# Attention's heads laid in pairs over the 128 rows: scores by row halves, mixing by column halves, and the first scores and the samples' q moved

## The chip, the cores and the metric

The kernel runs on one core of a Trainium2 chip. The metric is the device time of one launch in microseconds (us), lower is better. The core has five engines with instruction queues of their own: TensorE (PE, its weight loads shown as PEld), VectorE (DVE), ScalarE (ACT), GpSimd (POOL) and the queue that issues most DMAs (SP). They work in parallel and hand over to each other by semaphores.

## What is computed

One inference step of a two-layer decoder for 512 prompt tokens and 8 samples of 8 new tokens (576 tokens, 1024 features). Layer 0 is a recurrent block, layer 1 is attention over a window of 128 tokens; each ends with a retrieval of experts that takes most of the time. The change touches the attention alone: 16 query heads of 64 features, 4 key/value heads (so four query heads share one), a rotary position code on q and k, and a learned sink per head.

```python
def swa_prompt(q, k, v, sinks):           # blocks of 128 tokens, keys of the block and of the one before
    ...
    s = jnp.einsum('bnqkgd,bnskd->bnkgqs', qb, kb).astype(jnp.float32) * scale
    p = sink_softmax(s, mask[None, :, None, None], sink)
    o = jnp.einsum('bnkgqs,bnskd->bnqkgd', p.astype(v.dtype), vb)
    return o.reshape(b, t, N_HEADS * HEAD_DIM)
```

`sink_softmax` takes the larger of the row's maximum and the sink, exponentiates, and divides by the sum with the sink's own term. The samples do the same against 128 cached keys and their own 8.

## The kernel before, in words

Every engine has its program written out by hand; what sets the order of the work is the order of the code of each engine, and the semaphores between them. There is no scheduler.

Attention comes in the middle of the launch. TensorE projects k (two tiles of 128 features, `D_K`), v, and then q (eight tiles, `D_Q`, L1632). As each tile of q comes out of PSUM, ScalarE makes a copy with the halves of each head exchanged (`rope_shift`, L894), and VectorE's `rope` (L1402) multiplies that copy by the sine (L1407), the tile by the cosine (L1408), and adds the two into `qR`: once for the even head in the tile's rows 0 to 63 (L1412) and once for the odd head in rows 64 to 127 (L1413). Both go to rows 0 to 63 of `qR`, which is 64 rows by 16 heads by 576 tokens. After the last tile VectorE copies the samples' part of `qR` to `qS` (L1429).

Then come 16 **units**, one for each of 4 blocks of 128 prompt tokens and 4 key/value heads, in a software pipeline. For unit u:

- TensorE `scores` (L1842): 4 matmuls of 64 rows by 128 columns of weights, one per head, over 256 keys (128 for the first four units), to two PSUM banks.
- VectorE `scale_max`: scales and masks the scores (L1443), takes the maximum (L1450), and three small steps. ScalarE takes the exponentials (L914). VectorE `normalise` (two small steps and L1467).
- TensorE `turn`: 8 transposes (L1882). ScalarE copies them to `prT` (L924).
- TensorE `mix` (L1886): one matmul of 64 columns of weights for each of two blocks of keys (one for the first four units), over 512 columns, that is, four heads of 128 queries (L1893). All four heads come out in rows 0 to 63 of PSUM.
- VectorE `keep` (L1470): two copies of 64 rows, the even heads to rows 0 to 63 of `xn`, the odd ones to rows 64 to 127 (L1474).

A turn of TensorE's loop holds the scores of unit u+2, the transposes of unit u, the mixing of unit u-1, and, from u = 8 on, the mixing of one sample (`sample_mix`, L1917 and L1919). A turn of VectorE's loop holds the normalising of u, the scaling of u+2, and the copy of u-1. Two further items, 4 and 5, carry the samples' scores through the same ring of score banks, and VectorE does the samples' maximum, normalising and copies at fixed units. After the last unit the output projection starts (L1632 again).

The matmuls on `qR`, `kR`, `prT` and `vtok` are in plain fp32; the profile shows each of them as two instructions (so the 4 matmuls of a unit's scores stand as x8).

Of the kernel before, what the change touches and what calls it, by code (L numbers as in the profile page):

```python
# [25 lines left out]
P = 128  # L26
# [220 lines left out]
def decoder(nc, xin, consts, params, wts, wv, stconv, kcT, kc, vc, uT, u, v,  # L247
            yT, convP, hOut, kNew, vNewP, vNewS, kKeep, vKeep, convS, gate_dram, s_dram):
    with ExitStack() as ctx:
# [65 lines left out]
        atc = st.take("atc", [P, C_N - C_COS])  # L315
        qR = st.take("qR", [HD, NH, T])
        kR = st.take("kR", [HD, NKV, T])
        qS = st.take("qS", [HD, NB, NH, TS])
# [110 lines left out]
        def _(spq):  # L429
# [94 lines left out]
            spq.wait_ge(sem("k_ready"), 2)  # L524
            spq.dma_start(kNew, kR[:, :, TP - WIN:T]).then_inc(sem("out_done"), 16)
            load_weights(W_Q + 2, W_O + 2)
# [430 lines left out]
        def _(dve):  # L957
# [443 lines left out]

            def rope(d0, n, dst):  # L1402
# [12 lines left out]

            def attention():
                dve.wait_ge(sem("atc_loaded"), 16)
                norm_stats(2)
                norm_apply(N_KV, X_KV)
                rope(D_K, 2, kR)  # L1420
                dve.wait_ge(sem("roped"), 2)
# [4 lines left out]
                norm_apply(N_AT, X_AT, inv=rinv[:, :])  # L1426
                rope(D_Q, NC, qR)
                dve.wait_ge(sem("roped"), 2 + NC)
                dve.tensor_copy(qS[:, :, :, :], qR[:, :, TP:T].rearrange("p h (b s) -> p b h s", b=NB)  # L1429
                                ).then_inc(sem("qS_ready"), 1)  # L1430
                ob = xn
                dve.wait_ge(sem("tile_done"), D_O)

                def scale_max(k, u):
# [12 lines left out]
                    if not n:  # L1447
# [3 lines left out]
                    chain.settle()  # L1451
                    sk = prm[:, P_SINK + kv * GRP:P_SINK + (kv + 1) * GRP]
                    chain.did(dve.tensor_tensor(m[:, 0, 0:GRP], m[:, 0, 0:GRP], sk, ALU.max))
# [3 lines left out]
                    dve.tensor_tensor(m[:, 3, 0:GRP], sk, m[:, 0, 0:GRP], ALU.subtract  # L1457
                                      ).then_inc(sem("pmax"), 1)

# [10 lines left out]
                def keep(u):  # L1470
                    n, kv = divmod(u, NKV)
                    dve.wait_ge(sem("p_out"), u + 1)
                    for e in range(2):
                        ins = dve.tensor_copy(  # L1474
                            ob[e * HD:(e + 1) * HD, 2 * kv:2 * kv + 2, n * WIN:(n + 1) * WIN],
                            ps[0:HD, OUT, :].rearrange("p (g e q) -> p g e q", g=2, e=2)[:, :, e])
                        if e == 0:
                            chain.did(ins)
                    ins.then_inc(sem("o_copied"), 1)

# [52 lines left out]
                for k in items_due(-1):  # L1533
                    item(k)
                for u in range(UNITS):
                    normalise(u)
# [34 lines left out]
        def _(pe):  # L1571
# [255 lines left out]
            def attention():  # L1827
# [10 lines left out]
                project(W_Q, D_Q, NC, X_AT)  # L1838
                pe.wait_ge(sem("roped"), 2 + NC)
                pe.wait_ge(sem("v_ready"), 1)  # L1840

                def scores(k, u):  # L1842
                    n, kv = divmod(u, NKV)
                    ks = max(0, n - 1) * WIN
                    lo = 0 if n else WIN
                    for g in range(GRP):
                        ins = pe.matmul(sbank(k)[:, g // 2, (g % 2) * 256 + lo:(g % 2 + 1) * 256],
                                        qR[:, kv * GRP + g, n * WIN:(n + 1) * WIN],
                                        kR[:, kv, ks:(n + 1) * WIN], start=True, stop=True)
                    return ins  # L1850

                def sample_scores(k, h):
# [3 lines left out]
                    for b in range(4 * h, 4 * h + 4):  # L1856
                        for kv in range(NKV):
                            o = sbank(k)[32 * kv:32 * kv + 32, b // 2 % 2, (b % 2) * 256:(b % 2) * 256 + WIN + TS]
                            q = qS[:, b, kv * GRP:(kv + 1) * GRP].rearrange("p g s -> p (g s)")
                            pe.matmul(o[:, 0:WIN], q, kc_sb[:, b, kv], start=True, stop=True)  # L1860
                            ins = pe.matmul(o[:, WIN:], q, kR[:, kv, TP + b * TS:TP + (b + 1) * TS],
                                            start=True, stop=True)
# [23 lines left out]
                def mix(u):  # L1886
# [154 lines left out]
```

## Time and profile before

| | us |
|---|---|
| median of 3 runs | 3170.84 |
| lowest and highest | 3169.39, 3171.84 |
| the profiled execution, its own time | 3175.33 |
| its span | 3173.5 |
| from the last matmul of q's projection to the first of the output projection | 1642.1 to 1787.6 |
| granted TensorE clock over the span | 0.979 of full speed |

Durations below are of the profiled execution. Positions are us from the start of its span. PE's busy time of the whole span is 3063.0 us (97%) and DVE's 2544.1 us (80%); only a small window of the span belongs to the change.

### The profile page before, as it was taken

Reading aid. Unit: us, or ns where it says so; the run is one execution under the profiler, and the core shown is the slowest. Engines: PE = TensorE matmul, PEld = TensorE weight load, DVE = VectorE, ACT = ScalarE, POOL = GpSimd, SP = SyncE. Lnnn points to the kernel's source line nnn. Section 1 sums busy time; section 2 is a strip of 40 time slices with the busy share of each in tenths; the row PEclk is TensorE's granted clock in tenths of the full one; section 3 lists DMA queues with packets and bytes.
Section 4 is the critical chain, followed back from the end, with each engine's and each line's share of the span. In section 5 each row is a group of like instructions: output and inputs, shape, how many; then the busy total and the mean of one; then the engine's idle time right before and its main releaser. Section 6 shows DMA issues by size and latency. Waiting matters only on the chain.

```text
span 3173.5 us, 50434 instructions
## 1 busy us (share of the span) xinstructions
PE 3063.0 (97%) x19070; PEld 2973.1 (94%) x19070; DVE 2544.1 (80%) x4947; ACT 1379.8 (43%) x2558; POOL 1882.1 (59%) x1165
## 2 busy tenths in 40 slices
PE   8889999999999999999988899999999999999998
PEld 7779999999999999999875789999999999999998
DVE  7755999977776899989567448999877759998997
ACT  2522344477774333333344233343677753333333
POOL 4543488887776665664130233788877766565651
PEclk9999999999999999999987899999999999999999
DMA  3212499999999999999130022899999999999994
GB/s 111 73 54 92 139 335 347 325 403 393 394 386 367 401 401 398 400 395 398 58 99 1 27 67 85 283 348 347 355 400 394 387 360 398 401 398 400 400 397 191
DMA packets 286337, 920.89 MB, mean 290 GB/s; under 512 B 27344, under 2 KB 77136, under 8 KB 282432
## 3 DMA queue, kind: packets, MB, share of 16 engines
q1 hardware_dynamic: 154080, 415.37, 35.9%
q0 software_dynamic: 111280, 404.77, 33.3%
q10 hardware_dynamic: 20736, 97.53, 7.6%
q8 instruction: 152, 2.49, 0.3%
q14 instruction: 89, 0.73, 0.1%
HBM read 817.07 MB, written 102.38 MB: 290 GB/s over the span
## 4 chain that ended last, share of the span: by engine, by line
PE 67%; DVE 21%; DMA 8%; issue 2%; POOL 1%; ACT 1%; SPq 1%; DVEq 0%; ACTq 0%
PE ps L1767 24%; PE ps L1709 15%; PE ps L1632 10%; PE ps L1712 7%; DMA sring<-s_dram 6%; PE ps L1743 5%; DVE xrest L1168 2%; DVE xl L975 1%; DVE xn L982 1%; DMA gt<-gate_dram 1%; DVE low L1336 1%; DVE cand L1251 1%; DVE cand L1258 1%; DVE rowsB L1161 1%; PE ps L1893 1%
## 5 line engine op out<-in xcount | busy, mean ns | idle before, releaser
L787 ACT ACTIVATE high<-raw 128x1024 fp32r<-128x1024 f32 x512 | 542.8, 1060 | 937.2 <-PE ps L1767 640.2
L629 POOL TENSOR_TENSOR low<-raw,high 128x1024 fp32r<-128x1024 f32 x256 | 614.8, 2402 | 157.6 <-ACT high L787 154.2
L1709 PE MATMUL ps<-xh,high 128*128 128x384 f32 x2048 | 701.4, 342 | 6.3 <-ACT sring L840 6.3
L1767 PE MATMUL ps<-hh,high 128*128 128x384 f32 (+1 forms) x2048 | 691.4, 338 | 7.6 <-DVE low L1336 7.4
L1767 PE MATMUL ps<-hl,high 128*128 128x384 f32 x2048 | 691.7, 338 | 0.0
L1767 PE MATMUL ps<-hh,low 128*128 128x384 f32 x2048 | 690.7, 337 | 0.0
L1709 PE MATMUL ps<-xl,high 128*128 128x384 f32 x2048 | 688.6, 336 | 0.0
L620 POOL DMA_INDIRECT rowsB<-v,pick x192 | 330.0, 1719 | 207.1 <-DVE xrest L1168 192.3
L620 POOL DMA_INDIRECT rowsA<-v,pick x192 | 315.1, 1641 | 213.8 <-DVE xrest L1168 206.5
L1712 PE MATMUL ps<-xh,low 128*128 128x384 f32 x2048 | 399.5, 336 | 7.2 <-POOL low L629 7.2
L1767 PEld LDWEIGHTS ps<-hh,high 128*128 128x128 f32 x2048 | 385.2, 188 | 11.6 <-DVE low L1336 11.4
L1709 PEld LDWEIGHTS ps<-xh,high 128*128 128x128 f32 x2048 | 388.2, 190 | 7.2 <-ACT high L787 6.9
L1709 PEld LDWEIGHTS ps<-xl,high 128*128 128x128 f32 x2048 | 388.3, 190 | 0.0
L1767 PEld LDWEIGHTS ps<-hh,low 128*128 128x128 f32 x2048 | 385.4, 188 | 0.7
L1767 PEld LDWEIGHTS ps<-hl,high 128*128 128x128 f32 x2048 | 385.6, 188 | 0.0
L1712 PEld LDWEIGHTS ps<-xh,low 128*128 128x128 f32 x2048 | 360.8, 189 | 8.3 <-POOL low L629 8.2
L1336 DVE TENSOR_TENSOR low<-raw,high 128x1024 fp32r<-128x1024 f32 x256 | 311.2, 1216 | 0.0
L1632 PE MATMUL ps<-xh,high 128*128 128x288 f32 x1152 | 254.5, 303 | 26.8 <-DVE xl L975 18.4
L1161 DVE SCALAR_TENSOR_TENSOR rowsB<-rowsB,ps 128x1024 f32<-128x1024 f32 x192 | 230.6, 1212 | 34.5 <-DMA rowsB<-u,pick 34.2
L840 ACT ACTIVATE sring<-ps 128x384 f32<-128x384 f32 x256 | 125.1, 488 | 297.4 <-PE ps L1712 296.9
L1168 DVE SCALAR_TENSOR_TENSOR xrest<-rowsA,phid,xrest 128x1024 f32<-128x1024 f32 x192 | 249.0, 1297 | 0.6
L1323 DVE TENSOR_TENSOR sring<-sring,gt 128x384 f32<-128x384 f32 x256 | 140.4, 550 | 135.7 <-DMA sring<-s_dram 82.7
(282 smaller groups left out, 5205.3 us busy)
## 6 DMA issues: line engine op xcount, KB each, us to landing
raw<-uT SPq DMA_DIRECT2D x256, 512.0 KB, 6.8
raw<-v SPq DMA_DIRECT2D x256, 512.0 KB, 14.0
gate_dram<-gblk ACTq DMA_DIRECT2D x24, 2048.0 KB, 11.6
s_dram<-sring ACTq DMA_DIRECT2D x120, 384.0 KB, 6.8
gt<-gate_dram SPq DMA_DIRECT2D x30, 1536.0 KB, 20.9
sring<-s_dram SPq DMA_DIRECT2D x120, 384.0 KB, 14.7
raw<-wts SPq DMA_DIRECT2D x74, 512.0 KB, 3.3
rowsB<-u,pick POOLq DMA_INDIRECT x192, 8.0
```

Of the source, the lines that this page charges most:

```text
L620: pool.indirect_dma_start(out=row_slot(k), out_offset=None, in_=u if k < S0 + S1 else v, in_offset=bass.IndirectOffsetOnAxis(ap=pick[:, c: ...
L629: pool.tensor_tensor(low[:, m % 4], raw[:, m % 4], high[:, (m + 2) % 3].bitcast(F32), ALU.subtract).then_inc(sem("lo_ready"), 1)
L787: act.activation(high[:, (m + 2) % 3], tile_raw(m), ACT.Copy).then_inc(sem("hi_ready"), 1)
L1161: dve.scalar_tensor_tensor(row, row, 1.0, wide(XS0 if k < S0 else XS1), ALU.mult, ALU.mult, accum_out=phid[:, c:c + 1]).then_inc(sem("row_ ...
L1168: dve.scalar_tensor_tensor(acc[c >= S0], row.rearrange("p (c d) -> p c d", d=P), phid[:, c:c + 1], acc[c >= S0], ALU.mult, ALU.add).then_i ...
L1323: dve.tensor_tensor(hb, hb, gt[:, n // GE % 2, :, n % GE * GB:(n % GE + 1) * GB], ALU.mult).then_inc(sem("h_mul"), 1)
L1336: dve.tensor_tensor(tile_low(m), tile_raw(m), high[:, (m + 2) % 3].bitcast(F32), ALU.subtract).then_inc(sem("vlo_ready"), 1)
L1632: ins = pe.matmul(ps[:, dbank(d) + h, 0:H2], m[:, c], x[:, c, h * H2:(h + 1) * H2], start=(c == 0 and j == 0), stop=(c == NC - 1 and j == 2))
L1709: pe.matmul(ps[:, m % 2, 0:DN], a[:, c], x[:, c, 0:DN], start=(c == 0 and k == 0), stop=False)
L1712: ins = pe.matmul(ps[:, m % 2, 0:DN], b[:, c], xh[:, c, 0:DN], start=False, stop=(c == NC - 1))
L1743: ins = pe.matmul(ps[:, 2 + g % 2, i * P:(i + 1) * P], hotB[:, k], hotA[:, k], start=True, stop=True)
L1767: ins = pe.matmul(ps[:, c, 0:cols], w[:, c], h[:, n % 3, 0:cols], start=opens, stop=(n == KEYS - 1 and j == 2))
```

## The change

`qR` and `kR` now fill all 128 rows. `qR` holds a pair of heads per tile as the projection leaves it: the even head in rows 0 to 63, the odd one in rows 64 to 127. So `rope` makes one addition of 128 rows per tile of q where there were two of 64. `kR` holds each key head twice, once in either half of the rows, which takes four additions per tile of k where there were two.

`scores` takes the even head of a pair from rows 0 to 63 and the odd one from rows 64 to 127, in turn, into two different PSUM banks. A unit's slots are thereby ordered even heads first, and the sinks are read in that order. `mix` makes two matmuls over 256 columns where there was one over 512: the even heads' output goes to rows 0 to 63 of PSUM, the odd heads' to rows 64 to 127. `keep` is then a single copy of 128 rows.

The wait of TensorE for the tiles of q, which was for all eight ahead of the first scores, is now for seven ahead of the scores of units 0 to 2 and for all eight ahead of those of unit 3. The samples' copy to `qS`, now two copies, stands on VectorE behind the scaling of units 0 and 1.

```diff
-        qR = st.take("qR", [HD, NH, T])
-        kR = st.take("kR", [HD, NKV, T])
+        qR = st.take("qR", [P, NC, T])
+        kR = st.take("kR", [P, NKV, T])
...
-                    chain.did(dve.tensor_tensor(dst[:, 2 * f], rc[0:HD, r], rot[0:HD, r], ALU.add))
-                    ins = dve.tensor_tensor(dst[:, 2 * f + 1], rc[HD:P, r], rot[HD:P, r], ALU.add)
+                    if d0 == D_K:
+                        for e in range(2):
+                            rows = slice(e * HD, (e + 1) * HD)
+                            for at in range(2):
+                                ins = dve.tensor_tensor(kR[at * HD:(at + 1) * HD, 2 * f + e], rc[rows, r], rot[rows, r],
+                                                        ALU.add)
...
+                    else:
+                        ins = dve.tensor_tensor(qR[:, f], rc[:, r], rot[:, r], ALU.add)
                     ins.then_inc(sem("roped"), 1)
...
-                dve.wait_ge(sem("roped"), 2 + NC)
-                dve.tensor_copy(qS[:, :, :, :], qR[:, :, TP:T].rearrange("p h (b s) -> p b h s", b=NB)
-                                ).then_inc(sem("qS_ready"), 1)
...
-                    for e in range(2):
-                        ins = dve.tensor_copy(
-                            ob[e * HD:(e + 1) * HD, 2 * kv:2 * kv + 2, n * WIN:(n + 1) * WIN],
-                            ps[0:HD, OUT, :].rearrange("p (g e q) -> p g e q", g=2, e=2)[:, :, e])
...
+                    dve.tensor_copy(ob[:, 2 * kv:2 * kv + 2, n * WIN:(n + 1) * WIN],
+                                    ps[:, OUT, 0:2 * WIN].rearrange("p (g q) -> p g q", g=2)
+                                    ).then_inc(sem("o_copied"), 1)
...
                 for k in items_due(-1):
                     item(k)
+                dve.wait_ge(sem("roped"), 2 + NC)
+                by_half = qS[:, :, :, :].rearrange("p b (f e) s -> p b f e s", e=2)
+                for e in range(2):
+                    ins = dve.tensor_copy(by_half[:, :, :, e], qR[e * HD:(e + 1) * HD, :, TP:T]
+                                          .rearrange("p f (b s) -> p b f s", b=NB))
...
-                pe.wait_ge(sem("roped"), 2 + NC)
                 pe.wait_ge(sem("v_ready"), 1)
...
-                    for g in range(GRP):
-                        ins = pe.matmul(sbank(k)[:, g // 2, (g % 2) * 256 + lo:(g % 2 + 1) * 256],
-                                        qR[:, kv * GRP + g, n * WIN:(n + 1) * WIN],
-                                        kR[:, kv, ks:(n + 1) * WIN], start=True, stop=True)
+                    if u < NKV:
+                        pe.wait_ge(sem("roped"), 2 + (NC - 1 if u < NKV - 1 else NC))
+                    for g in range(2):
+                        for e in range(2):
+                            ins = pe.matmul(sbank(k)[:, e, g * 256 + lo:(g + 1) * 256],
+                                            qR[e * HD:(e + 1) * HD, 2 * kv + g, n * WIN:(n + 1) * WIN],
+                                            kR[e * HD:(e + 1) * HD, kv, ks:(n + 1) * WIN], start=True, stop=True)
...
-                        ins = pe.matmul(ps[0:HD, OUT, :], vtok[:, n - 1 + kb, kv * HD:(kv + 1) * HD],
-                                        prT[:, u % 2, 4 * kb:4 * kb + 4].rearrange("p g q -> p (g q)"),
-                                        start=(kb == kbs[0]), stop=(kb == 1))
+                        for e in range(2):
+                            j = 4 * kb + 2 * e
+                            ins = pe.matmul(ps[e * HD:(e + 1) * HD, OUT, 0:2 * WIN],
+                                            vtok[:, n - 1 + kb, kv * HD:(kv + 1) * HD],
+                                            prT[:, u % 2, j:j + 2].rearrange("p g q -> p (g q)"),
+                                            start=(kb == kbs[0]), stop=(kb == 1))
```

Two places of the engines' own order show what stands in a row before and now. The first is VectorE at the end of q's rope: `rc` and `rot` are the two products, `pr` the scores of a unit, `sm` its small sums. Before:

```order
L1407 TENSOR_TENSOR rot<-rot,atc 128x576 [waits rot_ready]
L1408 TENSOR_TENSOR rc<-ps,atc 128x576
L1412 TENSOR_TENSOR qR<-rc,rot 64x576 [waits d_free,dve_chain]
L1413 TENSOR_TENSOR qR<-rc,rot 64x576
L1429 COPY qS<-qR 64x1024 [waits roped]
L1443 SCALAR_TENSOR_TENSOR pr<-ps,atc 128x4x128 [waits p_scores,tile_done]
L1448 MEMSET pr 128x4x128
L1450 TENSOR_REDUCE sm<-pr 128x4 [waits dve_chain]
```

And now, up to the normalising of unit 0:

```order
L1421 TENSOR_TENSOR qR<-rc,rot 128x576 [waits d_free,dve_chain]
L1448 SCALAR_TENSOR_TENSOR pr<-ps,atc 128x4x128 [waits p_scores,tile_done]
...
L1464 TENSOR_TENSOR sm<-prm,sm 128x4 [waits dve_chain]
L1540 COPY qS<-qR 64x64x8 [waits roped]
L1540 COPY qS<-qR 64x64x8
L1469 TENSOR_TENSOR sm<-sm 128x4 [waits pexp]
L1471 RECIPROCAL sm<-sm 128x4 [waits dve_chain]
L1473 TENSOR_TENSOR pr<-pr,sm 128x1024 [waits dve_chain]
```

One addition is gone from each tile of q, and the copy to `qS` has moved behind the scaling of two units.

The second is TensorE in a turn of the loop that holds a sample too (scores, transposes, mixing, then the sample's mixing). Before:

```order
L1847 MATMUL ps<-kR,qR 128x256 [waits pmax]
L1847 MATMUL ps<-kR,qR 128x256 x3
L1882 MATMUL ps<-cst,pr 128x128 [waits prT_ready,p_ready]
L1882 MATMUL ps<-cst,pr 128x128 x7
L1893 MATMUL ps<-prT,vtok 64x512 [waits o_copied,prT_ready]
L1893 MATMUL ps<-prT,vtok 64x512
L1917 MATMUL ps<-pssT,vc_sb 64x32
L1919 MATMUL ps<-pssN,vnew 64x32
```

And now:

```order
L1907 MATMUL ps<-prT,vtok 64x256 [waits o_copied,prT_ready]
L1907 MATMUL ps<-prT,vtok 64x256 x3
L1932 MATMUL ps<-pssT,vc_sb 64x32
L1934 MATMUL ps<-pssN,vnew 64x32
```

The scores and transposes stand as before (L1859 and L1894 now), and the two matmuls over 512 columns have become four over 256; no semaphore has moved in the loop.

## Rows read from the trace of the kernel before

**Rows 1.** The page's chain that ended last, shares of the span by engine.
```profile
PE 67%; DVE 21%; DMA 8%; issue 2%; POOL 1%; ACT 1%; SPq 1%; DVEq 0%; ACTq 0%
```

**Rows 2.** Stretches: length, busy PE, PEld, DVE, ACT, POOL, granted clock, DMA share, GB/s.
```profile
1642.10:1656.80 14.70, 5.85 (x24) 5.26 (x24) 10.11 (x19) 6.01 (x14) 3.38 (x2) 0.62 0.56 142
...
1656.80:1786.20 129.40, 111.50 (x560) 68.55 (x560) 88.09 (x174) 51.95 (x156) 0.00 (x0) 0.76 0.02 9
```

**Rows 3.** VectorE's waits in 1656.8 to 1786.2: total us, times, longest.
```profile
DVE xn L1474 <- PE ps L1893: 23.2, 11, 4.7
DVE pr L1443 <- PE ps L1847: 13.0, 9, 4.7
```

**Rows 4.** The chain at the start of the stage: start, us, what.
```profile
1644.72 1.54 DVE rot L1407
...
1647.81 0.77 DVE qR L1413
1648.62 2.09 PE ps L1847 x8
1650.81 0.69 DVE pr L1443
```

**Rows 5.** Timeline of VectorE: start, us, line, tiles, shape, [idle before, releaser].
```profile
1584.52 0.06 DVE L1424 MEMSET mark<- 128x1 f32 x1 [11.05 <-PE ps L1834]
...
1648.60 0.69 DVE L1429 COPY qS<-qR 64x1024 f32<-64x1024 f32 x1
```

**Rows 6.** VectorE's copies by line and shape: count, busy us, mean ns, idle before.
```profile
L1474 DVE COPY xn<-ps 64x256 f32<-64x256 f32 x32 | 13.3, 417 | 23.8 <-PE ps L1893 23.2
```

**Rows 7.** The chain in the units, at full and at half clock.
```profile
1740.73 1.92 PE ps L1847 x8
1742.65 1.02 PE ps L1882 x8
1743.68 1.86 PE ps L1893 x4
...
1755.88 0.35 PE ps L1919 x2
...
1756.93 3.71 PE ps L1847 x8
1760.64 1.90 PE ps L1882 x8
```

**Rows 8.** Another stretch of the chain: mixing at half clock.
```profile
1727.29 3.60 PE ps L1893 x4
```

**Rows 9.** Timeline of VectorE in the units: the long waits and one short.
```profile
1684.52 0.86 DVE L1474 COPY xn<-ps 64x256 f32<-64x256 f32 x2 [0.97 <-PE ps L1893]
...
1703.18 0.86 DVE L1474 COPY xn<-ps 64x256 f32<-64x256 f32 x2 [2.68 <-PE ps L1893]
...
1730.93 0.87 DVE L1474 COPY xn<-ps 64x256 f32<-64x256 f32 x2 [2.42 <-PE ps L1893]
...
1760.68 1.23 DVE L1443 SCALAR_TENSOR_TENSOR pr<-ps,atc 128x1024 f32<-128x1024 f32 x1 [4.71 <-PE ps L1847]
1765.74 0.86 DVE L1474 COPY xn<-ps 64x256 f32<-64x256 f32 x2 [1.99 <-PE ps L1893]
1772.96 0.87 DVE L1474 COPY xn<-ps 64x256 f32<-64x256 f32 x2 [4.69 <-PE ps L1893]
1780.06 0.87 DVE L1474 COPY xn<-ps 64x256 f32<-64x256 f32 x2 [4.57 <-PE ps L1893]
1783.61 0.87 DVE L1474 COPY xn<-ps 64x256 f32<-64x256 f32 x2 [2.68 <-PE ps L1893]
```

**Rows 10.** TensorE by line and shape (rows*columns of weights, then moving): count, busy us.
```profile
L1719 PE MATMUL ps<-cst,xn 128*64 128x128 f32 x64 | 6.7, 276 | 0.0
...
L1798 PE MATMUL ps<-xn,ones 128*32 128x128 f32 x128 | 3.9, 273 | 0.0
```

**Rows 11.** Timeline of weight loads: the first load of a mixing behind transposes.
```profile
1727.22 0.29 PEld L1893 LDWEIGHTS ps<-prT,vtok 128*64 128x64 f32 x2 [0.33 <-issue]
```

More of the change, by code:

```diff
@@ L524, in _ @@
             spq.wait_ge(sem("k_ready"), 2)
-            spq.dma_start(kNew, kR[:, :, TP - WIN:T]).then_inc(sem("out_done"), 16)
+            spq.dma_start(kNew, kR[0:HD, :, TP - WIN:T]).then_inc(sem("out_done"), 16)
             load_weights(W_Q + 2, W_O + 2)
@@ L1400, in experts, with rope @@
                 dve.memset(mark[:, :], 0.0).then_inc(sem("x_ready"), 1)
-            def rope(d0, n, dst):
+            def rope(d0, n):
                 for f in range(n):
@@ L1411, in rope @@
                     dve.wait_ge(sem("d_free"), d + 1)
-                    chain.did(dve.tensor_tensor(dst[:, 2 * f], rc[0:HD, r], rot[0:HD, r], ALU.add))
-                    ins = dve.tensor_tensor(dst[:, 2 * f + 1], rc[HD:P, r], rot[HD:P, r], ALU.add)
+                    if d0 == D_K:
[4 more added lines that the diff above has]
+                                                        ALU.add)
+                                if (e, at) != (1, 1):
+                                    chain.did(ins)
+                    else:
+                        ins = dve.tensor_tensor(qR[:, f], rc[:, r], rot[:, r], ALU.add)
                     ins.then_inc(sem("roped"), 1)
@@ L1419, in attention @@
                 norm_apply(N_KV, X_KV)
-                rope(D_K, 2, kR)
+                rope(D_K, 2)
                 dve.wait_ge(sem("roped"), 2)
@@ L1426, in attention @@
                 norm_apply(N_AT, X_AT, inv=rinv[:, :])
-                rope(D_Q, NC, qR)
-                dve.wait_ge(sem("roped"), 2 + NC)
-                dve.tensor_copy(qS[:, :, :, :], qR[:, :, TP:T].rearrange("p h (b s) -> p b h s", b=NB)
-                                ).then_inc(sem("qS_ready"), 1)
+                rope(D_Q, NC)
                 ob = xn
@@ L1451, in scale_max, with pairs @@
                     chain.settle()
-                    sk = prm[:, P_SINK + kv * GRP:P_SINK + (kv + 1) * GRP]
-                    chain.did(dve.tensor_tensor(m[:, 0, 0:GRP], m[:, 0, 0:GRP], sk, ALU.max))
+                    sk = prm[:, P_SINK + kv * GRP:P_SINK + (kv + 1) * GRP].rearrange("p (g e) -> p e g", e=2)
+                    def pairs(i):
+                        return m[:, i, 0:GRP].rearrange("p (e g) -> p e g", e=2)
+                    chain.did(dve.tensor_tensor(pairs(0), pairs(0), sk, ALU.max))
                     chain.settle()
@@ L1456, in scale_max @@
                     chain.settle()
-                    dve.tensor_tensor(m[:, 3, 0:GRP], sk, m[:, 0, 0:GRP], ALU.subtract
-                                      ).then_inc(sem("pmax"), 1)
+                    dve.tensor_tensor(pairs(3), sk, pairs(0), ALU.subtract).then_inc(sem("pmax"), 1)
                 def normalise(u):
@@ L1472, in keep @@
                     dve.wait_ge(sem("p_out"), u + 1)
-                    for e in range(2):
-                        ins = dve.tensor_copy(
-                            ob[e * HD:(e + 1) * HD, 2 * kv:2 * kv + 2, n * WIN:(n + 1) * WIN],
-                            ps[0:HD, OUT, :].rearrange("p (g e q) -> p g e q", g=2, e=2)[:, :, e])
-                        if e == 0:
-                            chain.did(ins)
-                    ins.then_inc(sem("o_copied"), 1)
+                    dve.tensor_copy(ob[:, 2 * kv:2 * kv + 2, n * WIN:(n + 1) * WIN],
+                                    ps[:, OUT, 0:2 * WIN].rearrange("p (g q) -> p g q", g=2)
+                                    ).then_inc(sem("o_copied"), 1)
                 def sample_scale(k, h):
@@ L1534, in attention @@
                     item(k)
+                dve.wait_ge(sem("roped"), 2 + NC)
[3 more added lines that the diff above has]
+                                          .rearrange("p f (b s) -> p b f s", b=NB))
+                    if e == 0:
+                        chain.did(ins)
+                ins.then_inc(sem("qS_ready"), 1)
                 for u in range(UNITS):
@@ L1860, in sample_scores @@
                             pe.matmul(o[:, 0:WIN], q, kc_sb[:, b, kv], start=True, stop=True)
-                            ins = pe.matmul(o[:, WIN:], q, kR[:, kv, TP + b * TS:TP + (b + 1) * TS],
+                            ins = pe.matmul(o[:, WIN:], q, kR[0:HD, kv, TP + b * TS:TP + (b + 1) * TS],
                                             start=True, stop=True)
```

## The prediction

> **What bounds the kernel now.** The chain that ended last is TensorE work for two thirds of the span [rows 1], but nearly all of it is projections and experts, which the change leaves alone. So I read only the window of attention. The table of stretches cuts it in two: a start of 14.7 us in which TensorE is busy for 5.85, and the 129.4 us of the 16 units, with TensorE busy 111.5, VectorE 88.1, ScalarE 52.0 and a mean granted clock of 0.76 [rows 2]. The clock has two levels, 2.4 and 1.2 GHz, so about half of the units' time runs at the lower one. The reader should see there that two engines share the lead: VectorE works 88 us and TensorE makes it wait. The list of waits gives the amount: 23.2 us for the mixing and 13.0 us for scores, in 20 waits, 36.2 us in all [rows 3]. ScalarE is behind both. The end of the stage is the last copy of VectorE, so the stage lasts as long as VectorE's work, plus those 36.2 us, plus the start.
>
> The chain in the units gives one turn of the loop at either level of the clock [rows 7, 8]: scores 1.92 us at full speed and 3.71 at half, transposes 1.02 and 1.90, mixing 1.86 and 3.60. A pair of the samples' small matmuls is 0.35 us at half speed, and there are 8 pairs in a turn.
>
> **The start.** q's last tile leaves TensorE at 1642.1. VectorE multiplies from 1644.72 (that start is set by ScalarE's copies), adds, and ends at 1648.58; only then do the scores of unit 0 run, 2.09 us at half clock for two units' worth, and VectorE's first scaling begins at 1650.81 [rows 4]. Now the scores of units 0 and 1 need tile 6 only, which is roped before the projection ends, so they run at 1642.1 while VectorE still works on tile 7. One of the two last additions goes, and scaling starts at 1647.81: 3.0 us earlier. An addition over 128 rows might cost 1.54 us, as the multiplication L1407 over 128 rows does [rows 4], and not 0.77; then 0.8 of the 3.0 goes back. I take 0.77, since the elements per row are the same as in the additions of 64 rows. The copy to qS took 0.69 us under the first scores, where it cost nothing [rows 5]; two halves of it, 0.75 with the gap, now stand on VectorE with no cover, ahead of the first normalising. The start gains 3.0 - 0.75 = **2.3 us**.
>
> The two added additions per tile of k are 4 x 0.77 = 3.1 us on VectorE. They lie ahead of a wait of 11.05 us for v's projection [rows 5] and cost nothing; without that cover they would cost 3.1. The seven other additions saved in q lie under the projection and gain nothing.
>
> **VectorE's copies.** A unit's two copies take 0.87 us together, and each 0.42 for 256 elements a row [rows 6, 9]. One copy of 128 rows has the same 256 elements: 0.42. That is 0.45 x 16 = **7.2 us** of VectorE work.
>
> **TensorE's halves.** The scores are still 4 matmuls of the same length. The mixing is twice as many, half as long, so the same sum if nothing overlaps: for both the lower bound of the gain is nothing. What the trace shows of matmuls side by side: instructions that all write the same column half take 6.7 us for 64, or 105 ns each; of the same 128 columns moved, those that change quarter each time take 3.9 us for 128, or 30 ns each [rows 10]. That is 3.4 to 3.5 of a possible 4, and 3.8 without the tail of the two groups. So column halves in turn should come to some 0.53 of the time: mixing 0.98 us for 1.86, and 1.9 for 3.60. For row halves no row exists; the bounds are 1.92 (none) and 0.96 (all), and I take 1.02 for the nearest case, the columns, and 1.95 at half clock. A turn thus saves TensorE 1.8 us at full and 3.5 us at half clock.
>
> **What is left of VectorE's waits.** Thirteen of the 20 are of 1.62 us or less and sum to 36.2 - 23.7 = 12.5; the other seven (2.68, 2.42, 4.71, 1.99, 4.69, 4.57, 2.68) sum to 23.7 [rows 9]. I take the clock as it was at each. The small ones go, except that the first units mix one block only, and a wait like the 0.97 at 1684.5 keeps some: 1.1 us left in all. The long ones lose the half of the mixing or the scores just before them: 1.74, 1.74, 1.8, 1.5, 1.4, 1.3, 0.9, leaving 0.9, 0.7, 2.9, 0.5, 3.3, 3.3 and 1.8, or 13.4. The last three are a chain of normalise, transpose, mix, copy with no scaling left to fill it, so they stay at any clock. VectorE arrives 0.43 us earlier at each of the seven, which adds 3.0. Left: 1.1 + 13.4 + 3.0 = 17.5, so **18.7 us** of waits go.
>
> **The sum** is 2.3 + 7.2 + 18.7 = 28.2 us. The profiled execution took 3175.3, which becomes 3147.1; it lay 4.5 above the median of 3170.84, so for the median I say **3142.6 us**. After attention nothing is changed: the output projection starts at half clock now and will again. VectorE becomes the engine that bounds a turn: 1.6 (normalise) + 3.0 (scale) + 0.45 (copy) = 5.1 us of work against TensorE's 1.0 + 1.0 + 1.0 and 1.8 for a sample.
>
> **Rivals.**
>
> *Row halves do not overlap*, column halves do. For it: both halves write all 128 rows of PSUM, and no row of this trace has such a pair. Against it: they go to two banks. Then TensorE saves only 0.9 or 1.7 per turn, the waits for scores (13.0) stay as they are and those for the mixing lose about 10 while VectorE comes earlier: gain 2.3 + 7.2 + some 6 = 15.5, **3155 us**. If neither overlapped, VectorE's earlier arrival would be given back at the 20 waits, up to 20 x 0.45 = 9.0 of 9.5: gain 0.5 to 4.
>
> *The clock stays at half.* TensorE has less to do per turn; in the start, where it was busy 5.85 of 14.7 us, it had 0.62 [rows 2]. At half clock throughout, a turn with a sample is 1.95 + 1.9 + 1.9 + 8 x 0.35 = 8.6 us against VectorE's 5.1, so 3.5 of wait in each of six turns, some 13 in the last two turns and the end, and 1.2 in each of the first eight (1.6 + 1.9 + 1.9 + 0.45 and handovers make 6.3): 21 + 13 + 10 = 44 to 49 in place of 36.2. The gain is 9.5 - 8 to 9.5 - 13: +1.5 to -3.5, **about 3171 us**. Against it: at half clock TensorE would be all but fully busy, and out of just such a stretch it came back: mixing took 3.60 us at 1727.3 and 1.86 at 1743.7 [rows 7, 8]. At full clock throughout only the last three waits and 2 us more stay, 8.5 in all: gain 2.3 + 7.2 + 27.7 = 37, **3134 us**.
>
> *Slower: each change of half empties the array.* The first weight load of a mixing behind the transposes stood idle for 0.33 us at half clock [rows 11]; if alternating halves paid that for each change, nothing would overlap, and a unit has six changes, so 16 x 6 x 0.33 = 32 us at half clock, half that at full, some 24. Less the 0.5 to 4 that is left without overlap, and with a part under VectorE's work: slower by about 15, **3186 us**. It decides from a price of 4 / 96 = 0.04 us a change. Against it: the quarters of [rows 10] change at every matmul and run at 30 ns. The Trainium skill, "TensorEngine Tiling (Array Packing)", section "Key Properties", says that changing the tiling mode drains TensorE, but not changing the tile. By that rule the change adds no drain between halves; the trace's 30 ns agree.
>
> *It does not do what it says*: the order of each engine shows that it does; no chance of its own.
>
> **How the numbers follow.** Forecast (both overlap, clock mixed, gain 20 to 37): 0.73. Rows do not overlap: 0.13. Clock mostly at half: 0.09, of which a third is still faster. Drains: 0.05, nearly all slower. A measurement of this kernel tells 0.2%, 6.3 us, from no change. Faster: 0.73 + 0.13 + 0.03 = 0.89; same 0.06; slower 0.05. The range runs from full clock throughout, 3134, to a little above the case of rows alone, 3158; beyond lie the other two cases, 0.14.
>
> **What would show it.** In the profile after: the four matmuls of a unit's scores end in 1.0 us at full clock (1.9 if rows fail), four of a mixing in 1.0; the first scaling at about 1647.8, normalising of unit 0 at 1654.5; VectorE's waits 17 us in place of 36, the last three of them still there; the first matmul of the output projection near 1759 and not 1787.6; the clock of the units between 0.7 and 0.9. The prediction is wrong if the scores' instructions do not overlap, or if the granted clock falls below 0.65.

## The result and the profile after

| | before | after |
|---|---|---|
| median | 3171.34 (4 runs, 3169.39 to 3178.40) | 3133.06 (4 runs, 3130.48 to 3135.20) |
| ratio, 95% interval | | 0.9875 [0.9857, 0.9893] |
| span of the profiled execution | 3173.5 | 3133.4 |
| up to the end of q's projection | 1642.04 | 1633.28 |
| stage: from there to the output projection's first matmul | 145.53 | 112.09 |
| output projection | 52.4 | 53.7 |
| what follows | 1333.5 | 1334.3 |

The medians are 38.3 us apart in this comparison, where 28.2 was forecast; 3133.06 lies 0.9 us below the forecast's low end. The spans of the two profiled executions are 40.1 us apart, and the table splits that: 33.4 us come from the stage that the change touches, 8.8 from what runs ahead of it, and 2.1 go the other way behind it. A second comparison, of the same kernel under the name after_again, gave 3135.74 us against 3166.80 and a ratio of 0.9897 [0.9878, 0.9916], or 32.6 us.

The 8.8 us lie ahead of every instruction that the change touches. The first of those is in the rope of k, and the projection of k, which comes before it, starts 8.76 us earlier already (before, then after):

```profile
1551.01 0.51 PE L1632 MATMUL ps<-xh,high 128*128 128x288 f32 x2 [1.30 <-DVE xl L975]
1542.25 0.51 PE L1642 MATMUL ps<-xh,high 128*128 128x288 f32 x2 [1.30 <-DVE xl L975]
```

From there to the end of q's projection both take 91.03 us, so the additions of the changed rope cost and gain nothing there.

The stretches of after, columns as in [rows 2]: the stage, the stretch behind 1656.8, and the 17 us from the normalising of unit 0 on.

```profile
1633.28:1745.37 112.09, 79.86 (x640) 57.56 (x641) 89.93 (x176) 59.15 (x172) 3.38 (x2) 0.79 0.10 30
...
1656.80:1745.00 88.20, 69.66 (x542) 49.53 (x534) 69.98 (x137) 44.70 (x132) 0.00 (x0) 0.85 0.00 1
...
1645.81:1663.00 17.19, 14.08 (x172) 11.52 (x172) 13.52 (x28) 7.68 (x27) 0.00 (x0) 0.50 0.28 111
```

TensorE's busy time in the stage was 117.37 us and is 79.86; VectorE's was 99.17 and is 89.93, and VectorE now is the engine with more to do. The granted clock was 0.76 in the units [rows 2] and is 0.81 from the normalising of unit 0 on: the first 17 us of that run at exactly half speed, and half speed lasts until 1665.

The chain that ended last, answering to [rows 7] (start, us, what), with scores L1859, transposes L1894 and mixing L1907:

```profile
1702.54 1.09 PE ps L1859 x8
1708.66 1.09 PE ps L1894 x8
1709.75 1.01 PE ps L1907 x8
...
1725.83 2.03 PE ps L1859 x8
...
1732.95 1.09 PE ps L1894 x8
1734.04 1.04 PE ps L1907 x8
```

Scores take 1.09 us for 1.92 at full clock and 2.03 for 3.71 at half, mixing 1.01 for 1.86; the transposes, which the change leaves alone, take 1.09 for 1.02. So a pair of row halves runs in 0.55 to 0.57 of the time, a pair of column halves in 0.54.

VectorE's waits from 1655 to 1745, answering to [rows 3] (us, times, longest), and the ones at the end, answering to [rows 9]:

```profile
DVE xn L1479 <- PE ps L1907: 7.8, 5, 2.3
DVE pr L1448 <- PE ps L1859: 4.4, 2, 3.2
DVE pss L1486 <- PE ps L1873: 1.6, 2, 1.3
```

```profile
1727.88 1.23 DVE L1448 SCALAR_TENSOR_TENSOR pr<-ps,atc 128x1024 f32<-128x1024 f32 x1 [3.24 <-PE ps L1859]
...
1735.11 0.42 DVE L1479 COPY xn<-ps 128x256 f32<-128x256 f32 x1 [2.21 <-PE ps L1907]
...
1739.28 0.42 DVE L1479 COPY xn<-ps 128x256 f32<-128x256 f32 x1 [2.21 <-PE ps L1907]
1741.98 0.42 DVE L1479 COPY xn<-ps 128x256 f32<-128x256 f32 x1 [2.27 <-PE ps L1907]
```

They were 36.2 us in 20 waits and are 13.8 in 9; 17.5 were forecast. VectorE's copies out of the units, answering to [rows 6] (count, busy us, mean ns, idle before), halve:

```profile
L1479 DVE COPY xn<-ps 128x256 f32<-128x256 f32 x16 | 6.7, 421 | 8.0 <-PE ps L1907 7.8
```

The start, VectorE's timeline, answering to [rows 4]: last addition, first scaling, the copies to `qS`, and the first step of normalising unit 0.

```profile
1638.26 0.76 DVE L1421 TENSOR_TENSOR qR<-rc,rot 128x576 f32<-128x576 f32 x1
1638.93 0.69 DVE L1448 SCALAR_TENSOR_TENSOR pr<-ps,atc 128x512 f32<-128x512 f32 x1
...
1644.92 0.86 DVE L1540 COPY qS<-qR 64x512 f32<-64x512 f32 x2
1645.81 0.16 DVE L1469 TENSOR_TENSOR sm<-sm 128x4 f32<-128x4 f32 x1
```

Normalising begins 12.5 us after q's projection, where it was 14.8. An addition of 128 rows takes 0.76 us, the lower of the two prices considered. So the stage's 33.4 us are 2.2 at the start, 22.4 of waits, 6.6 of copies (13.3 to 6.7), and 2.2 that are left over. Of these, 1.8 are VectorE's busy time again: behind the first normalising it fell from 88.99 to 80.62 us, by more than the copies, and the durations of its instructions add up to only 6.7 less, so they overlap more in the record.

### The profile page after: what moved, and what is told of

Same layout as the page of the kernel before. It is cut to its first block, busy times and chain, and to the rows that moved or that the text cites. A ratio compares the mean times of both kernels' runs of the same rounds, so it can differ in the third digit from the quotient of the medians.

```text
span 3133.4 us, 50529 instructions
## 1 busy us (share of the span) xinstructions
PE 3022.0 (96%) x19126; PEld 2954.6 (94%) x19126; DVE 2526.3 (81%) x4928; ACT 1377.6 (44%) x2558; POOL 1879.4 (60%) x1165
## 4 chain that ended last, share of the span: by engine, by line
PE 74%; DVE 17%; DMA 5%; POOL 2%; issue 1%; ACT 1%; SPq 0%; DVEq 0%; ACTq 0%
PE ps L1777 30%; PE ps L1719 16%; PE ps L1642 11%; PE ps L1722 8%; PE ps L1753 5%; DMA sring<-s_dram 3%; DVE xl L975 1%; DVE xn L982 1%; POOL low L629 1%; DMA gt<-gate_dram 1%; DVE cand L1251 1%; DVE cand L1258 1%; DVE xrest L1168 1%; DVE slot L1264 1%; DVE rowsB L1161 1%
## 5 line engine op out<-in xcount | busy, mean ns | idle before, releaser
L1161 DVE SCALAR_TENSOR_TENSOR rowsA<-rowsA,ps 128x1024 f32<-128x1024 f32 x192 | 230.5, 1212 | 27.7 <-DMA rowsA<-u,pick 27.3
L1642 PE MATMUL ps<-xh,low 128*128 128x288 f32 x1152 | 248.1, 297 | 0.0
## 6 DMA issues: line engine op xcount, KB each, us to landing
gate_dram<-gblk ACTq DMA_DIRECT2D x24, 2048.0 KB, 12.5
```

The source lines that it names most:

```text
L1161: dve.scalar_tensor_tensor(row, row, 1.0, wide(XS0 if k < S0 else XS1), ALU.mult, ALU.mult, accum_out=phid[:, c:c + 1]).then_inc(sem("row_ ...
L1642: ins = pe.matmul(ps[:, dbank(d) + h, 0:H2], m[:, c], x[:, c, h * H2:(h + 1) * H2], start=(c == 0 and j == 0), stop=(c == NC - 1 and j == 2))
```

## The experiments

Two questions. Where do the 38.3 us come from: is the time outside the stage part of the change's worth? And is the stage's gain what the prediction says it is: row halves, column halves and one copy, the start, and a clock that does not fall? My theory was that the stage's gain is the pairs' overlap seen through VectorE's waits, and that the rest is scatter. The rivals: a gain outside the stage that repeats; one half of the change doing all; the clock doing most. "The stage" is always the stretch of the table above; it is read from the profiled execution, while ratios come from runs of both kernels in turn on one chip.

### The same kernels again

after_again is the changed kernel with no edit.

> The changed kernel once more, in five rounds, to measure what of its gain lies outside the stage of attention. In the profiles so far the stage (last matmul of q's projection to first of the output projection) went from 145.5 to 112.1 us, 33.4 less, while the work ahead of the stage, which is the same code, was 8.8 us shorter. Theory: that part is scatter between executions, so the stage stays at 112 within 2 us, the gain by rounds comes to 34 to 38 us, and the last matmul of q's projection ends anywhere in 1633 to 1642 us. Rival, the changed program makes the work ahead of it faster: q's projection ends near 1633 again and the gain is 38 to 42 us.

Measured: 3135.74 us, a ratio of 0.9897; stage 112.53, and 1634.21 ahead of it. The runs of before beside it went from 3158.19 to 3175.31, with a median of 3166.80. before_again is the kernel before with no edit.

> The kernel before once more, one look. The work ahead of the stage is the same code in all kernels; over the profiles so far its end lies at 1642.1 in the kernel before and at 1633.3, 1634.2 and 1639.8 in the changed ones. Theory (scatter between executions): the stage is 145.5 us within 1 and the end of q's projection anywhere in 1630 to 1645. Rival (the changed program is faster ahead of the stage): q's projection ends at 1640 or later again.

Measured: 3174.91 us in its one run; the stage took 145.68, 0.15 from the first, and q's projection ended at 1642.46, again late.

That second number is also what a repeated gain ahead of the stage would give, and in all ten profiles of changed kernels q's projection ended earlier, between 1633.28 and 1640.14. The ratios speak against such a gain: over the nine kernels of this section that have a ratio, the gain by ratio less the gain of the stage (145.53 less its own) lies between +3.3 (rows_in_turn) and -7.6 (filled), with a mean of -1.6 us; the first comparison, by its ratio 39.6 us, gives +6.2. A steady 5 to 9 us ahead of the stage would stand in that mean. Both profiled executions of before happened to be long ones, at 3175 us, where its medians are 3166 to 3171.

The traces add where the difference lies. In eleven of the twelve, k's projection to the end of q's takes 91.02 to 91.05 us, whatever the kernel does in rope; only its start moves, from 1542.02 to 1551.43. So no instruction of the change takes part in the 8.8 us; an indirect cause, such as where the program lies, no run excludes. Its start already varies by 7 us among changed kernels whose code up to there is the same. What makes that code vary stays open.

### Mixing and its copy undone

```diff
-                        for e in range(2):
-                            j = 4 * kb + 2 * e
-                            ins = pe.matmul(ps[e * HD:(e + 1) * HD, OUT, 0:2 * WIN],
-                                            vtok[:, n - 1 + kb, kv * HD:(kv + 1) * HD],
-                                            prT[:, u % 2, j:j + 2].rearrange("p g q -> p (g q)"),
-                                            start=(kb == kbs[0]), stop=(kb == 1))
+                        ins = pe.matmul(ps[0:HD, OUT, :], vtok[:, n - 1 + kb, kv * HD:(kv + 1) * HD],
+                                        prT[:, u % 2, 4 * kb:4 * kb + 4].rearrange("p g q -> p (g q)"),
+                                        start=(kb == kbs[0]), stop=(kb == 1))
```

`keep` is two copies of 64 rows again.

> The changed kernel with mixing as before: one matmul over 512 columns into rows 0 to 63, and two copies of 64 rows per unit. The scores stay in row halves. Theory (the overlap of column halves and the single copy both count): 14 to 18 us slower than the changed kernel, so 3147 to 3151 us; a mixing takes 1.86 us at full clock and 3.6 at half. Rival (VectorE bounds the stage, the overlap is hidden): only the copies' 0.45 x 16 = 7 us come back, 3140 us.

Measured: ratio 0.9954 [0.9934, 0.9974], 3153.93 us, 18 us above after_again; the stage took 126.68, 14.6 above after's, and a mixing 1.86 us at full clock again. That is as the theory says for the stage, while the median lies a little above the 3147 to 3151 expected. Column halves and the single copy together are worth about 15 us; no run parts the two.

### Scores undone

```diff
-                                            qR[e * HD:(e + 1) * HD, 2 * kv + g, n * WIN:(n + 1) * WIN],
-                                            kR[e * HD:(e + 1) * HD, kv, ks:(n + 1) * WIN], start=True, stop=True)
+                                            qR[:, kv * GRP + 2 * g + e, n * WIN:(n + 1) * WIN],
+                                            kR[:, kv, ks:(n + 1) * WIN], start=True, stop=True)
```

`qR` and `kR` have 64 rows and `rope` its two additions, as before the change; all else is as after.

> The changed kernel with q and k in rows 0 to 63 as before, so the four matmuls of a unit's scores use the same row half; slots, mixing in column halves and the single copy stay. Theory (the overlap of row halves counts in its own right): 8 to 12 us slower than the changed kernel, 3141 to 3145 us, scores 1.9 us at full clock. Rival (scores are hidden under VectorE's work once the mixing is short): under 4 us slower.

Measured: ratio 0.9960 [0.9943, 0.9976], 3156.33 us; the stage took 132.13, 20.0 above after's and well beyond what I expected. The stage's row and three rows of its chain:

```profile
1640.14:1772.27 132.13, 107.53 (x641) 78.31 (x641) 91.28 (x178) 59.17 (x172) 3.38 (x2) 0.69 0.09 25
```

```profile
1738.22 3.71 PE ps L1852 x8
1741.93 1.90 PE ps L1887 x8
1743.83 1.93 PE ps L1900 x8
```

The granted clock is 0.69, less than in any other kernel here, before included. From 1722 to 1756 all of the chain's scores, transposes and mixings run at half speed, though TensorE is busy for 32.3 of these 34 us; in the same place after has one such stretch of some 7 us, around the scores at 1725.83. So two things differ from after: the scores are longer, and the clock is lower. The next experiment parts the two.

### Scores over all 128 rows, with zeros

```diff
-        qR = st.take("qR", [P, NC, T])
+        qR = st.take("qR", [P, NH, T])
...
-                                            qR[e * HD:(e + 1) * HD, 2 * kv + g, n * WIN:(n + 1) * WIN],
-                                            kR[e * HD:(e + 1) * HD, kv, ks:(n + 1) * WIN], start=True, stop=True)
+                                            qR[:, kv * GRP + 2 * g + e, n * WIN:(n + 1) * WIN],
+                                            kR[:, kv, ks:(n + 1) * WIN], start=True, stop=True)
```

Each head of q stands in its own half of the rows, and the other half holds zeros that VectorE writes under v's projection; not shown are `rope`'s two additions and the writing of the zeros. The scores are the same numbers and all rows are in use, but no two of them can run side by side.

> As undo_scores (no two scores side by side), but each head's q stands in its own half of the rows with zeros in the other, so a scores matmul uses all 128 rows and takes as long as one of 64. Run undo_scores lost 20 us of the stage where 8 to 12 had been expected, with long stretches at half clock. Theory (the granted clock falls with the rows that the scores use, so a score of half the rows keeps it low): stage 122 to 126 us, clock in it above that of undo_scores by 0.05 or more, scores 1.9 us at full clock. Rival (the clock goes only by how long TensorE is busy): the same stage as undo_scores, 132 us within 2.

Measured: ratio 0.9936 [0.9911, 0.9961], 3145.09 us. This time holds 1.4 us that are not in the stage: from k's projection to the end of q's it takes 92.40 us for 91.03.

```profile
1634.42:1759.68 125.26, 94.49 (x641) 72.49 (x641) 91.03 (x178) 59.28 (x172) 3.38 (x2) 0.77 0.09 27
```

```profile
1714.45 1.92 PE ps L1863 x8
1716.38 0.87 PE ps L1898 x8
1717.25 1.01 PE ps L1911 x8
```

The two kernels have the same number of matmuls of the same length, in the same order: 1.92 us for a unit's scores at full clock in both. With 64 rows the clock is 0.69 and the stage 132.1; with 128 rows, of which q's half are zeros, it is 0.77 and 125.3, as the theory said ahead of the run. The clock over the whole span points the same way in every execution: 0.978 to 0.982 in the eight executions of undo_scores, 0.983 to 0.988 in the four of scores_full_rows. So of the 20.0 us, some 6.9 go with the lower clock, and 13.2 (125.3 to 112.1) are the overlap. That the rows themselves set the clock is supported and not proven: samples_apart below shows that a small shift of work in time also moves it. (The addition that `rope` has twice again, 0.8 us in the start, is in that second amount.) VectorE's waits for scores and mixing from the first normalising to the end, of undo_scores and then of scores_full_rows (us, times, longest), sum to 31.2 and 24.6, against 12.2 in after:

```profile
DVE pr L1441 <- PE ps L1852: 20.3, 8, 5.0
DVE xn L1472 <- PE ps L1900: 10.9, 9, 2.3
```

```profile
DVE xn L1483 <- PE ps L1911: 13.0, 5, 4.4
DVE pr L1452 <- PE ps L1863: 11.6, 8, 3.8
```

### One half's scores after the other

```diff
-                    for g in range(2):
-                        for e in range(2):
+                    for e in range(2):
+                        for g in range(2):
```

The two even heads come first, then the two odd ones, so the half changes once in four matmuls instead of at each.

> The changed kernel with a unit's four scores in another order: both matmuls of rows 0 to 63, then both of rows 64 to 127, where the halves changed with every matmul. Theory (a matmul runs beside its neighbour only, one in flight per half): half of the overlap is lost, scores take 1.4 to 1.5 us at full clock for 1.09, and the kernel is 3 to 5 us slower, 3136 to 3138 us. Rival (TensorE looks further ahead): scores stay at 1.1 us and the time is the same.

Measured: ratio 0.9886 [0.9862, 0.9910]; stage 112.72, 0.6 above after's.

```profile
1710.59 1.10 PE ps L1859 x8
```

A unit's scores take 1.10 us, not the 1.4 or so that only the middle pair side by side would give. The profile shows each fp32 matmul as two instructions, and one change of half in a unit is enough for nearly the whole gain. The trace shows how the starts lie: the eight begin in four pairs, 0.013 to 0.014 us apart within a pair and 0.2 to 0.3 us from pair to pair (in after 0.006 to 0.007 within a pair), while in before and in undo_scores, where all use the same rows, they begin one by one, 0.2 to 0.3 us apart. So from the first on, a matmul of the second half starts beside one of the first, ahead of others of the first half that stand before it in the program. The records do not name the half, so this is inferred from the starts, and how TensorE does it stays open. For the prediction it means that the number of changes of half has no price, in either direction.

### The start undone

TensorE waits for all eight tiles of q ahead of the first scores, and the copies to `qS` stand ahead of the first scaling.

```diff
                 project(W_Q, D_Q, NC, X_AT)
+                pe.wait_ge(sem("roped"), 2 + NC)
                 pe.wait_ge(sem("v_ready"), 1)
...
-                    if u < NKV:
-                        pe.wait_ge(sem("roped"), 2 + (NC - 1 if u < NKV - 1 else NC))
```

> The changed kernel with the start as before: TensorE waits for all eight tiles of q ahead of the first scores, and VectorE copies the samples' q ahead of the first scaling. Theory: stage 2 to 3 us longer than 112.3, so 114.5 to 115.5, by the later start of the first scaling. Rival (the start is made up by shorter waits in the first units): within 1 us of 112.3.

Measured: ratio 0.9903 [0.9875, 0.9932]; stage 113.17, 1.1 above after's.

```profile
1643.18 0.87 DVE L1439 COPY qS<-qR 64x512 f32<-64x512 f32 x2
1644.55 0.69 DVE L1456 SCALAR_TENSOR_TENSOR pr<-ps,atc 128x512 f32<-128x512 f32 x1 [0.50 <-PE ps L1858]
...
1650.54 0.15 DVE L1477 TENSOR_TENSOR sm<-sm 128x4 f32<-128x4 f32 x1
```

The stage is within 1 us of the 112.3 that the rival stands on, and not 2 to 3 longer. Normalising of unit 0 begins 13.1 us after q's projection (1637.40), where it is 12.5 in after and 14.8 before. So of the start's 2.2 us the moves make only 0.6. The rest is the single addition (0.8) and the first scores, whose row halves overlap too: the first scaling comes 1.4 us behind the start of the copies here, and came 2.2 behind it before.

### Matmuls that only fill

To put a price on the clock, matmuls on constants into an unused bank are added where TensorE waits anyway (`keep_warm`, which the kernel uses elsewhere).

```diff
                     item(k)
+                keep_warm(8, WARM)
                 for u in range(UNITS):
...
+                    if u == 0:
+                        keep_warm(4, WARM)
                     turn(u)
...
+                    if u < 5:
+                        keep_warm(1, WARM)
...
                 mix(UNITS - 1)
+                keep_warm(4, 2)
                 project(W_O, D_O, NC, X_O)
```

> The changed kernel with matmuls of no use (fp32, 512 columns, into a free bank) where TensorE waits: 8 behind the scores of units 0 and 1, 4 behind those of unit 2, 1 in each of the next five turns, 4 ahead of the output projection. They keep the clock up. Theory (low clock still costs the changed kernel its waits in the first units and the first 5.5 us of the output projection): stage 109 us for 112.3, output projection 3 us shorter, 3130 us or 5 to 6 us faster than the changed kernel, granted clock in the stage 0.9 or more. Rival (the added matmuls delay the scores as much as the clock gives): the same time within 2 us.

Measured: 3136.25 us, ratio 0.9914 [0.9893, 0.9936], no gain over after_again's 0.9897 that the runs can tell, where 5 to 6 us were expected.

```profile
1636.89:1747.58 110.69, 91.24 (x683) 58.20 (x683) 89.69 (x176) 59.31 (x172) 3.39 (x2) 0.92 0.10 30
```

The clock goes from 0.79 to 0.92, the stage from 112.1 to 110.7, and the output projection from 53.7 to 51.4. That is 3.7 us in the profile, which is the quickest of six executions (3128.47), and less than the runs resolve. With the pairs in place a higher clock gives the stage little, 1.4 us: VectorE has 89.7 us of work in these 110.7.

### The samples' mixing without its wait

`sample_mix` waits once until VectorE has emptied the samples' bank, 2.4 us in after (TensorE's waits):

```profile
PE ps L1932 <- DVE xn L1521: 2.4, 1, 2.4
```

With samples 4 to 7 in rows 64 to 127 of that bank, from where VectorE's copy (not shown) then takes them, the wait has nothing to guard.

```diff
...
-                    elif b == 4:
-                        pe.wait_ge(sem("s_kept"), 1)
                     for kv in range(NKV):
-                        o = ps[0:HD, OUTS_B, (b % 4) * P + 32 * kv:(b % 4) * P + 32 * kv + 32]
+                        o = ps[b // 4 * HD:(b // 4 + 1) * HD, OUTS_B, (b % 4) * P + 32 * kv:(b % 4) * P + 32 * kv + 32]
```

> The changed kernel with one more step: the output of samples 4 to 7 goes to rows 64 to 127 of its PSUM bank, where that of samples 0 to 3 has rows 0 to 63, so TensorE no longer waits for VectorE's copy of the first four. In the changed kernel's profiles this wait was followed by half clock and by VectorE's longest wait for scores, 3.2 and 2.4 us. Theory: that wait and the cold stretch behind it go, stage 108 to 109.5 us for 112.3, 3 to 4 us faster than the changed kernel in the profile, 3131 to 3133 us. Rival (the chain moves to VectorE, which has the same work): stage within 1 us of 112.3.

Measured: ratio 0.9908 [0.9890, 0.9926]; stage 113.63, 1.5 longer than after's, where I expected it shorter. VectorE's waits show where the gain went:

```profile
1737.75 0.42 DVE L1479 COPY xn<-ps 128x256 f32<-128x256 f32 x1 [2.97 <-PE ps L1907]
...
1744.17 0.42 DVE L1479 COPY xn<-ps 128x256 f32<-128x256 f32 x1 [4.45 <-PE ps L1907]
...
1748.68 0.42 DVE L1479 COPY xn<-ps 128x256 f32<-128x256 f32 x1 [4.09 <-PE ps L1907]
```

```profile
1725.00:1752.24 27.24, 21.98 (x129) 15.52 (x127) 13.30 (x34) 9.08 (x25) 0.00 (x0) 0.64 0.00 1
```

The wait of 3.24 us for scores is gone, but the last three have grown from 6.7 us to 11.5: the clock in the last 27 us is 0.64, where the last 25 us of after have 0.83. Why it fell there is not settled by these rows. The next kernel has this edit and the filling matmuls, and with them a clock that is held up.

> The same with the matmuls of no use of run filled, which gave a stage of 110.7 for 112.3 and a projection behind it that started at full clock. Theory (the two gains are in different places and add up): stage 106.5 to 108 us, the output projection's first 10 us hold 76 matmuls and not 60, 3128 to 3131 us. Rival: once the clock is up, VectorE's own 90 us of work and the last three units' chain leave nothing to gain, stage 109 us or more.

Measured: ratio 0.9889 [0.9871, 0.9907]; stage 109.72 at a clock of 0.92, 1.0 below filled's and above the 106.5 to 108 of the theory, as the rival had it. So the wait is worth about 1 us in one profile each, once the clock is held. Against after_again the intervals overlap; no version is shown to beat the change.

## Why the prediction was right or wrong

**What bounds the kernel.** Right. The stage fell by 33.4 us, of which 31.2 are VectorE's own savings and waits, as the prediction counted it; and in filled, where TensorE's clock rose from 0.79 to 0.92, the stage gave only 1.4 us.

**The start, 2.3 us.** Right at the place it spoke of, 2.2 at the normalising of unit 0; the first scaling comes 3.1 us earlier behind q's projection, for 3.0 forecast. Of the 2.2 the two moves make 0.6, and undone they cost the stage 1.1. One row was misread without harm: the 2.09 us [rows 4] are the scores of unit 0 alone; those of units 0 and 1 took 3.78 us.

**The copies, 7.2 us.** 6.6 by busy time, and the gap between the two copies with it.

**TensorE's halves.** Right. Scores forecast at 1.02 and 1.95 us, measured 1.09 and 2.03; mixing 0.98 and 1.9, measured 1.01 and (in undo_scores) 1.93. The column halves of [rows 10] were a fair guide for row halves too.
**What is left of VectorE's waits, 17.5 us.** This term was mis-sized. 13.8 are left, so 22.4 went and not 18.7. The seven long waits were reckoned with the clock as it was at each, and the last three, with 9.7 us, were said to stay at any clock. They stayed, but at 6.7, which is 3.0 of the 3.7 us. Before, the transposes and the mixing in front of two of them ran at half clock in part or whole:

```profile
1768.33 1.81 PE ps L1882 x8
...
1775.55 1.97 PE ps L1882 x8
```

In after both take 1.09, at full. The prediction named the case in which the clock rises, and priced it only as the range's end. It gave no reason for a rise: from the first normalising on the clock went from 0.76 to 0.81, and scores_full_rows against undo_scores points at the rows in use. The other term without a price is the 2.2 us left over in the stage. With 3.7 from the waits, and 0.7 less from the copies and the start, they make the 5.2 us by which 33.4 passes 28.2.

**The range.** This is the step that, with the mis-sized waits, put the time outside. Its low end, 3134, was the case of full clock throughout, reckoned from a median of three runs of before. It held no term for the scatter of the 3000 us that the change does not touch. Runs of before later lay between 3155.44 and 3178.40. Of the 9.5 us between forecast and result, 5.2 are the stage (33.4 for 28.2) and some 4 are scatter. Neither alone would have passed the low end: 3170.84 less 33.4 is 3137.4, and 3142.6 less 4.3 is 3138.3. That the time fell 0.9 us outside is partly chance: repeated, the same kernel gave 3135.74, within the range.

**The rivals.** Row halves that do not overlap: refuted by 1.09 us; its sum of 15.5 was near what undo_scores gained without them, 12.7 by ratio and 13.4 in the stage. Clock at half: from 1638 to 1665 it was at half, longer than before's 20 us there, with TensorE busy for 17.3 of these 27 us, and then rose. Drains at each change of half: refuted by the same 1.09, and by rows_in_turn, where one change instead of three inside a unit's scores leaves their time as it was.

**What each part is worth**, taken out alone, in the stage: row halves 20.0, column halves and the single copy 14.6, the moves at the start 1.1. The sum of 35.7 is above 33.4, since undo_scores is not simply a step back towards before: its clock of 0.69 is below before's 0.75, and some 6.9 of the 20.0 go with the clock.

## What to carry to other kernels

Where heads of 64 features make matmuls over half of TensorE's rows or columns, laying two of them side by side nearly halves their time, and the two orders of halves tried here came out alike. Price such an edit at the waits of the engine that comes behind, at the clock that will be there and not the one that was, since the edit can move it: here scores over half of the rows went with a lower clock than the same scores over all. And give the range a term for how far executions of the untouched code lie apart, above all where the median before rests on three runs.

## What the runs showed of the hardware

- With the same matmuls in the same order, the granted clock in the stage was 0.69 with TensorE busy for 107.5 of 132.1 us (undo_scores, 64 rows), and 0.77 with 94.5 of 125.3 us (scores_full_rows, 128 rows, half of them zeros): the kernel whose TensorE was busy for the larger share had the lower clock. The Trainium skill, "TensorE: Matmul & The Clock Gate", section "Part 1: The HAM clock gate (the "warmup" mystery)", ties the clock to how busy TensorE has lately been and does not say that the rows in use count. Part of the larger share comes from the lower clock itself, at which a matmul takes longer.
- One change of half in four fp32 matmuls gave the same time as a change at each: 1.10 and 1.09 us, where four over the same rows took 1.92.
- Taking away a wait of TensorE of 2.4 us made the stage no shorter while the clock could fall (0.83 to 0.64 in the last stretch), and 1.0 us shorter with the clock held, in one profile each.
- The same code ahead of attention took 1542.02 to 1551.43 us in twelve executions, while the stage repeated within 0.15 us (before) and 0.44 us (after).
